# Prompt attention of a hybrid decoder step: value pairs as stationary operand, probabilities divided before they are turned

## What is computed

```python
s = jnp.einsum('bhqd,bhqskd->bhqsk', qi, kg).astype(F32) * scale
s = jnp.where(mask, s, -jnp.inf)
p = jax.nn.softmax(s.reshape(B, H, qb, -1), axis=-1).reshape(s.shape)
return jnp.einsum('bhqsk,bhqskd->bhqd', p.astype(vg.dtype), vg)
...
o_c = moba_attention(q_c, pos, k_all, v_all).reshape(B, L, W_BRANCH) * jax.nn.silu(z_c)
```

## Time and profile before

| | |
|---|---|
| Time, median of 3 runs | 1124.29 us (1123.60 to 1124.68) |
| The profiled execution | 1122.23 us, span 1120.4 us |
| Granted TensorE clock, mean of the span | 0.998 |
| PE busy | 1097.7 us (98%) |
| PEld busy | 886.8 us (79%) |
| DVE busy | 696.3 us (62%) |
| ACT busy | 353.1 us (32%) |
| POOL busy | 133.5 us (12%) |
| L1900 PE, 128*128 128x64, 96 records | 11.8 us |

### The profile page before, as it was taken

How to read it: one execution, slowest core, us unless ns; L and a number is a source line. 1 busy time by engine, 2 the same in 40 slices (tenths; PEclk the granted TensorE clock), 3 DMA queues, 4 the chain that set the end, 5 groups by cost and what they waited for, 6 DMA issues and landing times.

```text
span 1120.4 us, 23102 instructions
## 1 busy us (share of the span) xinstructions
PE 1097.7 (98%) x8920; PEld 886.8 (79%) x8920; DVE 696.3 (62%) x1577; ACT 353.1 (32%) x809; POOL 133.5 (12%) x223
## 2 busy tenths in 40 slices
PE   7999999999999999999999999999899999999998
PEld 5778787767777798889977778777677778888997
DVE  4675647666766646467556674667667665463856
ACT  1242222422333264310323332233223432534013
POOL 0211402020130000000001123120202111000000
PEclk9999999999999999999999999999999999999999
DMA  8733136521432775453356321545124338544431
GB/s 266 226 113 119 33 111 201 129 79 39 86 118 77 210 267 151 151 170 127 103 159 180 113 87 54 183 145 126 40 83 109 87 97 281 185 142 161 141 114 43
DMA packets 162456, 148.57 MB, mean 133 GB/s; under 512 B 41641, under 2 KB 144655, under 8 KB 162157
## 3 DMA queue, kind: packets, MB, share of 16 engines
q1 hardware_dynamic: 156692, 135.40, 40.2%
q0 software_dynamic: 3104, 8.39, 2.3%
q10 hardware_dynamic: 2552, 3.32, 0.9%
HBM read 135.42 MB, written 11.07 MB: 131 GB/s over the span
## 4 chain that ended last, share of the span: by engine, by line
PE 92%; DVE 3%; ACT 1%; issue 1%; DMA 1%; SPq 1%; DVEq 0%; ACTq 0%
PE psum L1297 48%; PE psum L1338 10%; PE psum L1359 7%; PE psum L1225 5%; PE psum L1549 2%; PE psum L1566 2%; PE psum L1413 1%; PE psum L1424 1%; PE psum L1685 1%; PE psum L1951 1%; PE psum L1900 1%; DMA arena<-in_cache_k 1%; PE psum L1769 1%; PE psum L1930 1%; PE psum L1576 1%
## 5 line engine op out<-in xcount | busy, mean ns | idle before, releaser
L1297 PE MATMUL psum<-x_b,ring 128*128 128x288 f32 x928 | 242.8, 411 | 0.0
L1297 PE MATMUL psum<-x_a,ring 128*128 128x288 f32 x928 | 242.8, 411 | 0.0
L1297 PEld LDWEIGHTS psum<-x_b,ring 128*128 128x128 f32 x928 | 170.1, 190 | 48.5 <-issue 6.2
L1297 PEld LDWEIGHTS psum<-x_a,ring 128*128 128x128 f32 x928 | 170.1, 190 | 48.5 <-issue 6.2
L2036 ACT ACTIVATE arena<-psum 128x512 f32<-128x512 f32 (+7 forms) x181 | 78.2, 452 | 172.2 <-PE psum L1225 62.2
L1297 PE MATMUL psum<-z,ring 128*128 128x288 f32 (+1 forms) x384 | 83.5, 368 | 0.0
L1297 PEld LDWEIGHTS psum<-z,ring 128*128 128x128 f32 x384 | 62.3, 190 | 12.8 <-issue 2.3
L2036 ACT ACTIVATE arena<-arena 128x256 f32<-128x256 f32 (+9 forms) x102 | 44.5, 464 | 62.5 <-DVE arena L3300 28.3
L1225 PE MATMUL psum<-consts,arena 128*128 128x128 f32 (+2 forms) x362 | 53.6, 279 | 7.4 <-DMA arena<-in_x_prompt 4.9
L1225 PEld LDWEIGHTS psum<-consts,arena 128*128 128x128 f32 (+2 forms) x362 | 42.6, 144 | 17.7 <-issue 6.3
L2036 ACT ACTIVATE triangles<-psum 128x512 f32<-128x512 f32 (+2 forms) x48 | 24.7, 515 | 76.0 <-PE psum L1549 57.0
(11 more groups left out here) (479 smaller groups left out, 1987.3 us busy)
## 6 DMA issues: line engine op xcount, KB each, us to landing
ring<-in_w_in SPq DMA_DIRECT2D x72, 1024.0 KB, 5.4
ring<-in_w_branch SPq DMA_DIRECT2D x12, 1024.0 KB, 5.5
arena<-in_cache_k SPq DMA_DIRECT2D x32, 256.0 KB, 3.1
arena<-in_cache_v SPq DMA_DIRECT2D x32, 256.0 KB, 3.6
ring<-in_w_out SPq DMA_DIRECT2D x8, 1024.0 KB, 5.2
ring<-in_w_pg SPq DMA_DIRECT2D x8, 1024.0 KB, 5.2
arena<-in_state_dn SPq DMA_DIRECT2D x8, 512.0 KB, 6.8
out_dn_sample<-arena POOLq DMA_DIRECT2D x8, 512.0 KB, 6.6
```

The source lines that it names most:

```text
L1297: ins = mm(out[:, 0:n], lhs, rhs(k), start=k == 0, stop=k == k_tiles - 1)
```

## The change

The values become the stationary operand. One matmul takes the values of two heads (128 channels) as weights, and the turned probabilities of these two heads (2 x 128 queries) as moving operand. Its output has channels on the partitions and 256 columns; of the four quarters the two in which channels and probabilities belong to the same head are used. The output is thus already turned, and `c_out` with its transposes is dropped; VectorE multiplies the halves, 64 partitions each, into Z from `c_pv`. As queries are now along the free axis of the output, the division by the sums moves ahead of the transposes: VectorE scales `CP` in `c_prob` and signals `c_p`, on which TensorE's `c_prob` waits in place of `c_e`. The entries of `FILL` of the dropped steps are added to those of the step behind, so the sequence of fillers and the remaining steps stays the same.

```diff
-    "c_done": {"c_out": (1, None)},
+    "c_done": {"c_pv": (1, None)},
...
-    "c_os": {"c_pv": (1, None)},
-    "c_ot": {"c_out": (1, None), "c_sout": (1, None)},
+    "c_p": {"c_prob": (1, None)},
+    "c_ot": {"c_sout": (1, None)},
...
         add("c_pv", t, g)
-        if g == 1:
-            add("c_out", t)
...
-        0, 7, 6, 3, 0, 1, 0, 1, 0, 4, 6, 3, 0, 6, 0, 4, 2, 3, 0, 9, 3, 6, 2, 4, 1, 0, 1, 13, 2, 10, 5, 2, 2]
+        0, 7, 6, 3, 0, 1, 0, 1, 0, 4, 6, 3, 0, 6, 0, 4, 5, 0, 9, 3, 6, 6, 1, 0, 1, 13, 2, 10, 5, 2, 2]
...
             def c_prob(l, t, g):
-                pe.wait_ge(S.sem("c_e"), S.count("c_e"))
-                pe.wait_ge(S.sem("c_done"), S.count("c_done"))
+                pe.wait_ge(S.sem("c_p"), S.count("c_p"))
...
             def c_pv(l, t, g):
                 pe.wait_ge(S.sem("c_pts"), S.count("c_pts"))
-                pe.wait_ge(S.sem("c_os"), S.count("c_os", S.at - 1))
-                for hd in range(4):
+                pe.wait_ge(S.sem("c_done"), S.count("c_done", S.at - 1))
+                for pr in range(2):
+                    out = M[4][:, 256 * pr:256 * pr + 256].rearrange("p (h n) -> p h n", h=2)
                     for st in range(t + 1):
-                        ins = mm(M[4][:, 64 * hd:64 * hd + 64], CPT[:, st, hd, :], CVN[:, st, 64 * (4 * g + hd):64 * (4 * g + hd) + 64],
-                                 start=st == 0, stop=st == t)
+                        a = 128 * (2 * g + pr)
+                        ins = mm(out, CVN[:, st, a:a + 128], CPT[:, st, 2 * pr:2 * pr + 2, :], start=st == 0, stop=st == t)
                 ins.then_inc(S.sem("c_o"), 1)
-
-            def c_out(l, t):
-                pe.wait_ge(S.sem("c_os"), S.count("c_os"))
-                for m in range(4):
-                    ins = tr(M[2][:, 128 * m:128 * m + 128], CON[:, 128 * m:128 * m + 128])
-                ins.then_inc(S.sem("c_ot"), 1)
...
             def c_prob(l, t, g):
                 dve.wait_ge(S.sem("c_e"), S.count("c_e"))
                 link(dve.reciprocal(CMX[:, 2, :], CMX[:, 1, :]))
+                p = CP[:, :, 0:128 * (t + 1)]
+                tt(p, p, bc(CMX[:, 2, :], 2, [128, 4, 128 * (t + 1)]), MUL).then_inc(S.sem("c_p"), 1)
+                dve.wait_ge(S.sem("c_p"), S.count("c_p"))
 
             def c_pv(l, t, g):
                 dve.wait_ge(S.sem("c_o"), S.count("c_o"))
-                dve.wait_ge(S.sem("c_ot"), S.count("c_ot"))
-                tt(CON[:, 256 * g:256 * g + 256].rearrange("p (h n) -> p h n", h=4),
-                      M[4][:, 0:256].rearrange("p (h n) -> p h n", h=4), bc(CMX[:, 2, :], 2, [128, 4, 64]), MUL).then_inc(S.sem("c_os"), 1)
-                dve.wait_ge(S.sem("c_os"), S.count("c_os"))
-
-            def c_out(l, t):
-                dve.wait_ge(S.sem("c_ot"), S.count("c_ot"))
-                stt(Z[:, 2, :, tok(t)], v4(M[2], 128), 0.5, Z[:, 2, :, tok(t)], MUL, MUL).then_inc(S.sem("c_done"), 1)
+                for hh in range(2):
+                    r, z = rows_of(hh), Z[rows_of(hh), 2, 2 * g:2 * g + 2, tok(t)]
+                    ins = stt(z, M[4][r].rearrange("p (q h n) -> p q h n", q=2, h=2)[:, :, hh, :], 0.5, z, MUL, MUL)
+                ins.then_inc(S.sem("c_done"), 1)
                 dve.wait_ge(S.sem("c_done"), S.count("c_done"))
```

More of the change, by code:

```diff
@@ L1380, in up_ready @@
                 else:
-                    pe.wait_ge(S.sem("c_done"), S.count("c_done", pos[("c_out", l, 1)]))
+                    pe.wait_ge(S.sem("c_done"), S.count("c_done", pos[("c_pv", l, 1, 1)]))
             def source(l, st):
@@ L1998, in _ @@
                       b_fin=b_fin, b_norm5=b_norm5, c_rms=c_rms, c_rope=c_rope, c_nat=c_nat, c_score=c_score,
-                      c_prob=c_prob, c_pv=c_pv, c_out=c_out, c_keys=c_keys, c_past=c_past, c_sprob=c_sprob, c_spv=c_spv, c_sout=c_sout, y_out=y_out, y_end=y_end)
+                      c_prob=c_prob, c_pv=c_pv, c_keys=c_keys, c_past=c_past, c_sprob=c_sprob, c_spv=c_spv, c_sout=c_sout, y_out=y_out, y_end=y_end)
             for i, st in enumerate(order):
@@ L3376, in _ @@
                       bs_scale=bs_scale, bs_pairs=bs_pairs, bs_in=bs_in, bs_sq=bs_sq, bs_w=bs_w, bs_u=bs_u, bs_y=bs_y, bs_out=bs_out,
-                      c_turn=c_turn, c_rope=c_rope, c_score=c_score, c_prob=c_prob, c_pv=c_pv, c_out=c_out, c_past=c_past, c_sout=c_sout,
+                      c_turn=c_turn, c_rope=c_rope, c_score=c_score, c_prob=c_prob, c_pv=c_pv, c_past=c_past, c_sout=c_sout,
                       y_out=y_out)
```

## The result

The changed kernel takes 1139.1 us (median of 4 runs, 1137.8 to 1141.2) against 1124.5 us (median of 4, 1123.6 to 1125.7) for the kernel before, run on the same chip. The ratio is 1.0123, with a 95% interval of 1.0104 to 1.0141: slower by 14.6 us. The forecast was 1142 us in a range from 1134 to 1147. The profiled execution took 1137.8 us (1122.2 before) with a span of 1136.0 us (1120.4 before), and its mean granted clock is 0.994 (0.998 before).

What follows compares the result with a forecast made beforehand. TensorE, busy 1097.7 of 1120.4 us, was taken as the bound. Stalls +14.9, removed transposes -1.8, product 0 and clock falls +5 gave +18 us: 1142 us, range 1134 to 1147.

Steps and rivals of the forecast that it cites:

- The stalls: TensorE idle ahead of the `c_prob` transposes, waiting for VectorE's scaling: 7.44 us in a layer, 14.9 us for both.
- The chain of the prediction: Ahead of `c_prob`: reciprocal 0.18 (or 0.17) us, 0.03 to the next instruction, scaling 0.69 or 1.22, 0.05 to TensorE.
- The product: `c_pv` in its new shape: 24 records of 256 columns, 5.2 us in a layer as before, so taken as 0.
- the removed transposes: `c_out` dropped: four transposes for each query tile, 0.44 us for four, 1.76 us less over both layers.
- The clock: Falls to half rate behind the four 2.72 us stalls: 1.7 us each, at most 6.8 us, taken as 5 us.
- Rival (a): Stalls at `c_prob` as worked out, but the clock holds: +13.1 us, 1137.4 us; chance 22%.
- I take nothing: What the stalls might give back: waits for cache keys are 0.7 us in all, so counted as zero.
- Rival (d): Part of the loss comes back through shortened waits or earlier end of `c_out`: +6 to +10 us; chance 5%.
- (e): A change lost in the noise, within 0.2% (2.2 us); stalls a tenth of those worked out; chance 2%.
- (b): Scaling done before TensorE reaches `c_prob`, so only the removed transposes count: -1.8 us, 1122.5 us; chance 3%.

Runs made afterwards that it cites:

- The doubled scaling: The changed kernel with a second multiplication of the probabilities, by ones, ahead of the scaling: 1152.2 us.
- the form alone: The changed kernel without the scaling, transposes waiting for the exponentials, output never divided by the sums: 1120.0 us, ratio 0.9956 to the kernel before.
- the scaling alone: The kernel before with probabilities scaled ahead of their transposes and the eviction a plain copy; product and `c_out` as before: 1144.7 us, ratio 1.0182.
- the one with one late fetch of 3.4 us: The changed kernel with more fillers ahead of the transposes and the scaling as its own VectorE step ahead of the last projections' evictions: 1125.8 us.

## Why the prediction was right

**The stalls.** Forecast 1.13, 0.87, 2.72 and 2.72 us in a layer, measured 1.14, 0.89, 2.72 and 2.73; 14.9 us for both layers, forecast and measured. The chain of the prediction (reciprocal, scaling, 0.05 us to TensorE) holds in each term, and so does its reading that in tile 1 the eviction of `p_up` is what makes the scaling late: with the order of the two turned around, the wait was 1.3 us less in one group and gone in the other. The doubled scaling shows that there is no slack behind it, as the prediction had it.

**The product.** A record of 256 columns was taken at 0.216 us. Four of them take 440.23 - 439.36 = 0.87 us and eight 455.25 - 453.53 = 1.72 us, so 0.215 to 0.218; one of the groups of four, at 0.97 us, is longer. 24 records of a layer take 5.3 us where 5.2 were forecast. Even, as said, and with the removed transposes the form alone is a gain, of which 1.76 us were forecast.

**The clock.** Taken at 5 us, measured at 5.0 us, by three falls where the sum allowed for up to four. The place agrees: at the end of the stall, with TensorE at work. Rival (a), dense work around the stalls holds the clock, had 22% and is refuted in three of four cases; the fourth, 2.57 us like the others and with the clock at 1.00 behind it, shows that it isn't certain either. By the time alone one could not tell: +14.6 us is nearer to the +13.1 of rival (a) than to the +18 of the forecast. It is the clock of the windows that decides. That the Trainium skill (TensorE: Matmul & The Clock Gate, The HAM clock gate) has activity release the fast clock agrees in direction with the windows of this trace; its table of states, read as strictly as the prediction tried it, would have left stalls between dense work out, and in three of four cases they counted.

That the 5 us came out is in part luck, because the row it was worked out from is no like case. In the kernel before, the windows give 1.00 up to 9 us, but eight transposes take twice as long there as in mid-run:

```profile
4.89 1.97 PE L1225 MATMUL psum<-consts,arena 128*128 128x128 f32 x8 [4.89 <-DMA arena<-in_x_prompt]
```

1.97 us stand here against 1.04 us: TensorE began at its lower clock, came up only at some 9 us and fell at 12.6 us. The rows nearer to the case are two idles that the kernel before has in mid-run, 1.81 and 1.65 us (waits of TensorE in the kernel before):

```profile
PE psum L1740 <- issue: 3.5, 2, 1.8
```

No fall stands behind either, and the prediction left them out. They say that an idle of that length in dense work need not bring a fall; that 2.57 us would, no row of before could tell.

**What was mis-sized.** By the prediction's own terms, 14.9 - 1.8 + 0.1 + 5.0 makes 18.2 us, and the spans differ by 15.6. The step that failed is "I take nothing" for what is given back. Laid side by side, the timeline of after gains on that of before 0.3 us at 249 us, 0.4 at 409 us, 1.4 at 800 us and 0.5 at 960 us. The first and third are the stops that the profile puts down to issue, 3.5 us before and 1.5 + 0.3 after; the second and fourth the waits for cached keys, 0.7 us before and 0.2 after. That is 2.6 us. The waits for keys moved by run (they are 1.9 us in the kernel with the form alone), so I don't claim a cause for those 0.5 to 0.9 us. Nor do I for the 0.3 us at 249 us, ahead of which the change alters nothing on TensorE; the kernel with the scaling alone has the shorter stop there too, 1.54 us. The 1.4 us at 800 us are shown to be an effect of the change: they went with 64 instructions and came back with them. The prediction could have seen the row: the stop of 1.65 us stands in the timeline of before, but its own text said that no idle in mid-run is longer than 0.7 us when another engine causes it, and looked no further at idle time that nobody causes.

Rival (d) has part of the right mechanism with the wrong size: something does come back, but 2.6 us, and the measured +14.6 is far from its +6 to +10. For (e) the prediction asks for stalls of a tenth; by its own sum up to 4.0 us of the 14.9 would have done, which changes nothing, as the rows left no room for either (b) or (e). The forecast of 1142 is 2.9 us above the measured time; by the spans 2.6 us are this term, of which 1.4 are shown to come from the change.

## What to carry to other kernels

When an operation moves ahead of a step that the bounding engine waits for, cost it by its place in the other engine's queue, not by its length: here 1.2 us of VectorE cost 2.7 us of TensorE, because 0.9 us of eviction stood ahead of it, and that eviction had itself to wait for TensorE. The cure is to put the operation ahead of whatever the bounding engine needs later, and to bring independent work in between; look first at what that work was covering, since in this kernel it was a fetch. Idle time that the profile puts down to "issue" deserves a look when instructions are removed: here it was 1.4 us of the result.

## What the runs showed of the hardware

- **Idle length and the clock.** In these runs idles of 3.8 us (four) and 3.4 us (one, for a DMA) all had a fall of the clock, idles of 2.56 to 2.57 us had one in six of eight cases (three of four in the kernel after, three of four with the scaling alone), and two of 2.29 us had none. None of the mid-run idles of 1.3 to 1.9 us had one either, whether for VectorE, for a DMA or put down to issue. A fall began between 1.7 us before the idle's end and 0.7 us after it. Most lasted 3.4 us and cost 1.4 to 1.7 us; two in the kernel with the scaling doubled lasted 6.8 us. So shortening an idle from 2.6 to 1.3 us saved more than the 1.3 us. The 1.64 us idle at the start, which had a fall behind it, doesn't fit into this by length alone; it is the one place where the clock had come up only 3 us earlier. Whether that is what sets it apart was not tested.
- **The start differs between executions.** In the profiles of three kernels (before, after and the one with one late fetch of 3.4 us) the clock is up at some 9 us and falls again at 12.3 to 12.6 us. In the other seven the first projection runs at 0.480 us for a record of 288 columns (0.243 at the upper clock) from its first records until 15 to 19 us. With that, the kernel with the form alone is 1.4 us behind the kernel before at 17 us, long before the change; a difference of 1 us between two profiled spans says nothing unless one looks where it arises.
- **A stop that goes by the count of instructions.** TensorE stops, idle with nothing in the profile to wait for, at a fixed number of records from the start: 1834 in layer 0, in all ten kernels, and 6268 to 6270 in layer 1, wherever the stop is seen. It costs 1.3 to 1.8 us (layer 0) when it falls into a run of 64 x 64 matmuls, 0.76 us for 38 records, that is 0.02 us a record against 0.11 to 0.24 elsewhere; 64 instructions fewer put it behind the run and it cost 0.3 us instead of 1.65. What TensorE waits for there, no run here shows.
